# Splitting one more output-projection tile by tokens, and moving the sums of squares one step on

## What is computed

```python
def layer_norm(x, g, b):
    xf = x.astype(jnp.float32)
    mu = jnp.mean(xf, axis=-1, keepdims=True)
    var = jnp.mean(jnp.square(xf - mu), axis=-1, keepdims=True)
    y = (xf - mu) * lax.rsqrt(var + LN_EPS) * g.astype(jnp.float32) + b.astype(jnp.float32)
    return y.astype(x.dtype)

def first_block(...):
    for l in range(DEPTH):
        if l < N_A_LAYERS:
            mix = diff_attention(...)          # ends in  o.reshape(b, s, D_MODEL) @ w_o
        else:
            ...
            mix = chunk_attention(...)         # ends in  o.reshape(b, s, D_MODEL) @ w_o
        x = layer_norm(DEEPNORM_ALPHA * x + mix, ln_g[l, 0], ln_b[l, 0])
        x = layer_norm(DEEPNORM_ALPHA * x + swiglu(x, ffn_w_in[l], ffn_w_out[l]), ln_g[l, 1], ln_b[l, 1])
    return x
```

## Time and profile before

| | us |
|---|---|
| median of 3 runs | 2656.29 |
| lowest and highest of them | 2656.26, 2656.71 |
| the profiled execution's own time | 2657.04 |
| its span, first to last instruction | 2655.2 |
| PE busy in the span | 2601.5 (98%) |
| DVE busy | 1360.1 (51%) |
| ACT busy | 1037.4 (39%) |
| mean granted TensorE clock | 0.997 |

### The profile page before, as it was taken

One profiled execution on the slowest core, in us unless ns is written; L12 is line 12 of the kernel. 1 busy time (PEld: TensorE's weight loads), 2 busy tenths in 40 slices (PEclk: granted clock), 3 DMA queues, 4 the chain that ended last, 5 costly groups with the idle time before them and its releaser, 6 DMA issues.

```text
span 2655.2 us, 42783 instructions
## 1 busy us (share of the span) xinstructions
PE 2601.5 (98%) x18948; PEld 2321.2 (87%) x18948; DVE 1360.1 (51%) x2195; ACT 1037.4 (39%) x1699; POOL 30.7 (1%) x69
## 2 busy tenths in 40 slices
PE   8999999999999999999999999999999999999998
PEld 6776888888877788888889899999999989999998
DVE  5766533324555653333567546555336754655523
ACT  4554522213444442221345345344224534443421
POOL 0000000000000000000000000000000000000000
PEclk9999999999999999999999999999999999999999
DMA  5221222222322122222231132222223113222222
GB/s 187 87 66 64 80 95 95 92 97 82 105 71 80 64 80 95 96 91 89 75 120 65 57 104 80 96 94 80 90 89 135 65 57 105 83 93 96 92 88 76
DMA packets 39466, 236.03 MB, mean 89 GB/s; under 512 B 5248, under 2 KB 7296, under 8 KB 17008
## 3 DMA queue, kind: packets, MB, share of 16 engines
q1 hardware_dynamic: 34912, 214.98, 24.0%
q0 software_dynamic: 3792, 17.26, 1.9%
q10 hardware_dynamic: 576, 1.05, 0.1%
HBM read 222.65 MB, written 6.42 MB: 86 GB/s over the span
## 4 chain that ended last, share of the span: by engine, by line
PE 91%; DVE 5%; ACT 2%; issue 0%; DMA 0%; DVEq 0%; ACTq 0%
PE P L522 77%; PE P L612 3%; PE P L634 3%; PE P L529 2%; DVE WL L1778 1%; PE P L977 1%; PE P L891 1%; PE P L646 1%; PE P L660 1%; ACT WH L1219 1%; PE P L689 1%; DVE X L2078 1%; DVE small L2081 1%; PE P L867 0%; ACT X L1432 0%; PE P L1027 0%
## 5 line engine op out<-in xcount | busy, mean ns | idle before, releaser
L522 PE MATMUL P<-XH,WL 128*128 128x264 f32 (+3 forms) x3080 | 848.3, 324 | 24.6 <-DVE XL L2468 9.6
L522 PE MATMUL P<-XL,WH 128*128 128x264 f32 (+3 forms) x3080 | 823.4, 316 | 0.0
L522 PE MATMUL P<-XH,WH 128*128 128x264 f32 (+3 forms) x3080 | 821.0, 316 | 0.0
L1778 DVE TENSOR_TENSOR WL<-raw,WH 128x1024 fp32r<-128x1024 f32 (+1 forms) x404 | 483.9, 1201 | 535.4 <-ACT WH L1219 535.0
L1219 ACT ACTIVATE WH<-raw 128x1024 fp32r<-128x1024 f32 (+1 forms) x404 | 418.0, 1038 | 598.0 <-PE P L522 594.1
L522 PEld LDWEIGHTS P<-XH,WL 128*128 128x128 f32 x3080 | 520.0, 188 | 73.5 <-DVE XL L2468 9.5
L522 PEld LDWEIGHTS P<-XH,WH 128*128 128x128 f32 x3080 | 519.0, 189 | 38.2
L522 PEld LDWEIGHTS P<-XL,WH 128*128 128x128 f32 x3080 | 518.9, 188 | 35.4
L2449 DVE SCALAR_TENSOR_TENSOR tmp<-P,PP,tmp 128x527 f32<-128x527 f32 (+1 forms) x88 | 66.8, 759 | 195.2 <-ACT tmp L1726 195.2
L522 PE MATMUL P<-GHH,WL 128*128 128x264 f32 (+1 forms) x704 | 149.1, 283 | 0.0
L522 PE MATMUL P<-GHL,WH 128*128 128x264 f32 (+1 forms) x704 | 148.8, 282 | 0.0
(11 more groups left out here) (338 smaller groups left out, 3412.2 us busy)
## 6 DMA issues: line engine op xcount, KB each, us to landing
raw<-in_wts SPq DMA_DIRECT2D x170, 1024.0 KB, 4.9
raw<-in_wts SPq DMA_DIRECT2D x32, 896.0 KB, 4.7
spill<-X POOLq DMA_DIRECT2D x2, 2112.0 KB, 8.8
X<-spill POOLq DMA_DIRECT2D x16, 264.0 KB, 3.1
tmp<-in_biasT POOLq DMA_DIRECT2D x16, 256.0 KB, 3.7
qswap<-qraw SPq DMA_DIRECT2D x44, 64.0 KB, 2.0
tab<-in_tR POOLq DMA_DIRECT2D x2, 1056.0 KB, 5.9
tmp<-tmp SPq DMA_DIRECT2D x20, 64.0 KB, 2.0
```

The lines of the kernel that those rows point to most:

```text
L522: ins = nc.tensor.matmul(P[:, a:a + x1 - x0], wb[:, s, 128 * k:128 * k + 128], xb[:, kx, x0 - c0:x1 - c0], start=start and i == 0, stop=st ...
L1778: nc.vector.tensor_tensor(WL[:, u % NS, 0:length(u)], raw[:, u // 2 % RAW, a:a + length(u)], WH[:, u % NS, 0:length(u)].bitcast(F), ALU.su ...
```

## The change

- The last three tiles of the two attentions' output projections (s = 0 and 2) are computed in halves, in place of the last two. Tile 5 uses the PSUM bank `ln_bank(s, 2)` for half 0 and bank 0 for half 1.
- `mean(0)` now stands in tile 5's half 1 (after its block 3) and `var(0, ...)` in tile 6's half 1 (after its block 4); nothing stands in tile 7's. Each mean takes the running sum over tiles 0 to 4 and three single tiles.
- `between` (s = 0, 1 and 2) puts the sums of squares of half 1 two after blocks 5, 6 and 7 of phase 0 and the last two after block 0 of phase 1.
- On DVE and ACT the weight units follow the tile loop, which is one shorter: unit u+8 is split where u+9 was, and u+9 moves into the loop over `normal` and `split`, ahead of `res(7, 1)`. `res(5, 1)` stands after the centring, `res(6, 1)` after `normal(2)` and `split(0)`.

```diff
-HALF_BANK = {(6, 0): 3, (7, 0): 4, (6, 1): 5, (7, 1): 6}
+def half_bank(s, m, hf):
+    return {(5, 0): ln_bank(s, 2), (5, 1): 0, (6, 0): 3, (7, 0): 4, (6, 1): 5, (7, 1): 6}[m, hf]
...
                 def beside(m, kt):
-                    if last == 2:
-                        if m == 6 and kt == 3:
+                    if last == 3:
+                        if m == 5 and kt == 3:
                             mean(0)
-                        elif m == 7 and kt == 2:
+                        elif m == 6 and kt == 4:
                             var(0, *range(8))
...
                         if k == 2:
                             mean(1)
-                        elif k >= 4:
-                            var(1, 2 * k - 8, 2 * k - 7)
+                        elif k >= 5:
+                            var(1, 2 * k - 10, 2 * k - 9)
+                    elif k == 0:
+                        var(1, 6, 7)
...
-                return layer_norm(s, tiles, ((u + 6,), (u + 7,)), oh, ol, META)
+                return layer_norm(s, tiles, ((u + 5,), (u + 6,), (u + 7,)), oh, ol, META)
...
                     result(m, 0)
-                    if last == 1 and m == 1:
+                    if m == 1:
                         highs(top + 2)
                     elif m == 3:
-                        highs(top + 4 - last)
+                        highs(top + 3)
...
-            layer_norm(0, 1, range(first["ao"], first["ao"] + 6), 2)
+            layer_norm(0, 1, range(first["ao"], first["ao"] + 5), 3)
...
                 centre(0, *range(8))
-                if last == 2:
-                    res(6, 1)
+                if last == 3:
+                    res(5, 1)
                 lows(top + 1)
...
                     if m >= 2:
                         split(m - 2, 0)
-                    if m == 3:
-                        if last == 1:
-                            lows(top + 2)
+                    if m == 2 and last == 3:
+                        res(6, 1)
+                    elif m == 3:
+                        lows(top + 2)
                         res(7, 1)
                     elif 5 <= m < 9:
                         centre(1, 2 * m - 10, 2 * m - 9)
-                lows(top + 4 - last)
+                lows(top + 3)
...
-            layer_norm(0, 1, [(first["ao"] + m,) for m in range(8)], 2)
+            layer_norm(0, 1, [(first["ao"] + m,) for m in range(8)], 3)
```

More of the change, by code:

```diff
@@ L779, in layer_norm @@
                     for m in range(8 - last, 8):
-                        b = HALF_BANK[m, hf]
+                        b = half_bank(s, m, hf)
                         take(b)
@@ L1754, in act_program @@
             tail(18, (group_b(3), 33))
-            layer_norm(2, 3, range(first["bo"], first["bo"] + 6), 2)
+            layer_norm(2, 3, range(first["bo"], first["bo"] + 5), 3)
             feed_forward(1)
@@ L1892, in res @@
                     a, b = HV[hf]
-                    x, pb = X[:, m, a:b], bank(HALF_BANK[m, hf])[:, a - META:b - META]
+                    x, pb = X[:, m, a:b], bank(half_bank(s, m, hf))[:, a - META:b - META]
                     dve.wait_ge(*(at("unit", tiles[m][-1]) if hf else at("uh", s, m)))
@@ L2478, in dve_program @@
             tail(18, (group_b(3), 33))
-            layer_norm(2, 3, [(first["bo"] + m,) for m in range(8)], 2)
+            layer_norm(2, 3, [(first["bo"] + m,) for m in range(8)], 3)
             feed_forward(1)
```

## The result

| | before | after |
|---|---|---|
| median, us (18 runs each) | 2656.83 | 2661.5 |
| lowest and highest, us | 2655.93, 2659.32 | 2659.5, 2663.57 |
| the profiled execution's own time, us | 2657.04 | 2659.5 |
| its span, us | 2655.2 | 2657.6 |

The changed kernel takes 1.0016 times as long as the one before, 95% interval 1.0009 to 1.0023. By the medians it is 4.67 us slower. The forecast was 2660.9, 4.6 above the median shown then (2656.29 of three runs), with a range of 2659.0 to 2662.9.

A forecast was written before the change was run, and what follows sets the result against it. PE, 91% of the chain ending last, was taken as the bound. Shifts of 1.8 (s = 0), 1.1 (s = 1) and 1.8 (s = 2) sum to 4.7 us; forecast median 2660.9, range 2659.0 to 2662.9.

The forecast's parts named there:

- More work on PE: s = 0 and 2: tile 5 in halves and a third single tile in each mean add 1.00 us.
- The first wait: Before the feed-forward's first matmul, s = 0 and 2: from 1.10 to 1.64 us, released by WL of u+9.
- The second wait goes, the third stays: s = 0 and 2: block 2's wait of 0.78 us goes; block 4's stays at 1.1.
- The hole of 0.66: s = 0, 1 and 2: moving the first pair of squares' sums opens a 0.66 us wait at block 5.
- Half 1's wait: Ahead of half 1's first feed-forward matmul: the wait grows from 0.2 to 0.5 us.
- The sum: Stage shifts: 1.8 us at s = 0, 1.1 at s = 1, 1.8 at s = 2, together 4.7.
- The clock: Whole kernel: as many half-clock spells as before, each costing 1.64 us.
- rival 2: One spell fewer: s = 2's half-clock spell goes and none comes, 2659.3 us; chance 0.12.
- rival 1: Slower by over 0.2%: one more half-clock spell, 2662.5 us (chance 0.30), or two more, 2664.2 (chance 0.05).
- only those at s = 2 led to a spell: Waits at s = 0 and s = 2 are alike, but only s = 2's preceded a half-clock spell, costing 1.64 us.
- The bound of 0.2%: Smallest difference a measurement tells from no change, 5.3 us: line at 2661.6; chance 0.40 over it, 0.59 within.
- Rivals 3 and 4: 3: block 5's hole costs nothing, 2657.6, chance 0.06; 4: the cover works, WL not holding PE, 2653, chance 0.04.

The follow-up runs named there:

- f4: Changed kernel with var(0) after tile 6's first k-block, half 1's mean behind block 1, its sums of squares behind blocks 3 to 6; 2648.61 us.
- f3: Kernel before with var(0) behind tile 6's half 1, half 1's mean behind block 1, its sums of squares behind blocks 3 to 6; 2647.9 us.
- e5: Kernel before with DVE's centring of half 1 one loop step later, behind normal(6) and split(4), at s = 0, 1 and 2; 2653.22 us.
- e1: Changed kernel with half 1's sums of squares put back behind blocks 4 to 7, three tiles in halves kept; 2658.47 us.
- e2: Kernel before with only half 1's sums of squares moved one block later, two tiles in halves kept; 2660.38 us.
- e3: Changed kernel with weight unit u+9 split one step earlier on ACT and DVE, ahead of res(6, 1), at s = 0 and 2; 2662.52 us.
- f5: f3 plus half 0's sums of squares behind block 8, not 11, of the last tile's half 1 at s = 1 and 3; 2645.93 us.
- f1: Kernel before with half 0's sums of squares, var(0), right behind tile 6's half 1 at s = 0 and 2; 2654.96 us.
- f2: Kernel before with half 1's mean behind block 1 and its sums of squares behind blocks 3 to 6, one block earlier; 2648.59 us.

## Why the prediction was right, step by step

- **More work on PE, 1.00 a stage: held.** `var(0)` began 263.58 - 248.76 = 14.82 after tile 5's start; the working had 263.93 - 249.08 = 14.85. f4 against f3 shows the whole price as 1.22, of which 0.23 is a wait.
- **The first wait becomes 1.64, released by WL of u+9: held.** 23.81 after tile 5's start, predicted 23.87. The row at s = 1, the same instruction in the same place, carried this; the longer cover alone would have said 271.31.
- **The second wait goes, the third stays: held.** But the reason given for the third ("centring, normal and split only begin behind mean(1)") was a matter of order on DVE, as e5 showed. It was read as fixed since the change doesn't touch it.
- **The hole of 0.66 at block 5, at three places: held to the digit** (0.66 at s = 0, 1 and 2), and shown by e1 and e2 to come from the moved sums alone. The 1.45 between two splits is 279.88 - 278.43 = 1.45 in the trace after.
- **Half 1's wait 0.2 to 0.5: held** (0.52).
- **The sum:** 1.85 (predicted 1.8) at s = 0, 1.09 (1.1) at s = 1. At s = 2, 39.91 against the 38.29 of before without its spell: 1.62 (1.8). This is the one term that came out smaller, and not by a wait: the stage of s = 2 ran at the faster pace, 0.23 less, and at the pace of before it would be 1.85 too. Together 4.56 of 4.7 as measured, 4.8 at one pace, and 4.67 by medians. The waits that the prediction lists for s = 0 after the change (1.64, 1.1, 0.66 and 0.5) add up to 3.9, not to the 4.0 that it states; measured they are 3.94, and 0.04 more at block 2. By parts the medians give 1.12 (expected 1.4) and 3.03 (expected 3.3). In absolute terms the median lies 0.6 above the forecast, mostly because the kernel before has a median of 2656.83 over 18 runs and 2656.29 was known.
- **The clock, "as many spells as before": not borne out by the profiled executions.** The spell at s = 2 that the trace of before showed did not come, which was rival 2's mechanism, and none came instead. So that one execution reads 2659.5, close to rival 2's 2659.3. Over all runs the medians moved by the sum of waits and work, so the typical number of spells seems unchanged; that they are the same ones is not shown. One more spell (rival 1) fits at most the three slowest runs. Nor do the waits at s = 2 alone bring the spell there, as "only those at s = 2 led to a spell" suggests: e2 has the same three (1.1, 0.8 and 1.1) and the hole besides, and kept full clock from tile 5 to half 1:

```profile
905.33:944.58 39.25, 35.88 (x237) 32.67 (x235) 25.36 (x55) 17.01 (x35) 0.00 (x0) 1.00 0.16 54
```

The bound of 0.2% lay 0.1 us from where the median came out: 2661.5 under a line at 2661.6; that it fell on this side was luck.
- **Rivals 3 and 4** (the hole costs nothing; the cover works) are refuted by the rows at 279.88 and 272.57.

What the prediction didn't look at is e3's lesson. It added waits one after the other, each by who released it. That was right for this change, since each wait was moved by a known step; it would have been wrong for a change that removes one. Bringing the feed-forward's start forward by 1.12 was worth nothing, while one earlier block for PE's sums took 2.3 us off a stage.

## What to carry to other kernels

Where two engines feed each other around a reduction, look for the instruction that waits for the other engine and for what is queued behind it: here DVE stood 1.60 us for a mean while the tile that PE needed next was queued behind, and one turn of a loop was worth 4 us. Place a reduction as early as its inputs allow before paying for more cover: three edited places gave 3.42 us a stage with no work added, while a third half tile cost 1.2 on top of them and gave no cover that was still needed. Before pricing the removal of a wait, follow the same queue to the next one; before moving sums later, ask which gap they were filling.

## What the runs showed of the hardware

The number and place of the spells at half clock differ even where the work ahead of them is the same. The profiled executions had them at 204 to 206 (before, changed, e1, e2, e3, f5), at 232 to 235 (e3, e5, f1 to f4), at 928 to 934 (before, e3) and at 1322 to 1344 (all but before, changed, e5 and f2). At the very end the clock is at half in all of them, behind the last matmul, where it costs nothing (from 2651.3 in the changed kernel, whose last matmul starts at 2648.5). Three of e3's, in the windows view:

```profile
203.95:210.80 6.85, 6.85 (x25) 4.47 (x25) 3.17 (x11) 2.55 (x10) 0.00 (x0) 0.50 0.14 59
234.70:238.10 3.40, 3.40 (x9) 2.63 (x10) 1.23 (x2) 1.81 (x2) 0.00 (x0) 0.50 0.00 0
934.40:937.80 3.40, 3.40 (x12) 2.88 (x13) 0.54 (x2) 0.50 (x1) 0.00 (x0) 0.50 0.22 94
```

Its profiled execution took 2666.36, 3.8 over its own median; the spells, four and one of them of double length, are the likely reason. All edits act later than 248, so whether a spell stands at 204 or at 233 was not decided by them. At 1.6 us apiece, one profiled execution can't tell a change of under 2 us; the length of a stage with no spell in it can, to about 0.2, and closer once the two paces of the half-0 matmuls are told apart (5.60 or 5.44 for 48 of them, 8.39 or 8.16 for 72).
